# TensorE's program for RWKV pairs 1 to 7: a loop against a written-out program

## The reference, cut to what matters

```
xn = RMSNorm(h)
h += W_o( sigmoid(gA) * RWKV7(xn) + sigmoid(gB) * GLA(xn) )
h += SwiGLU(RMSNorm(h));  y = RMSNorm(h)

RWKV7, per head of 64 (16 heads), token by token:
S_t = S_{t-1} (diag(w_t) - kk_t^T (a_t * kk_t)) + v_t^T k_t ;  o_t = S_t r_t
```

## Time and profile before

| | |
|---|---|
| median of 3 runs | 2993.82 us (2993.78 to 2996.28) |
| the profiled execution | 2995.29 us, of which 2993.7 us span |
| TensorE busy | 2721.7 us, 91% of the span |
| VectorE, ScalarE busy | 928.4 us, 637.5 us |
| mean granted TensorE clock | 0.93 of full |
| RWKV pairs, from the first matmul of pair 0's inverse to that of pair 7's | 749.8 to 1857.9 us |

### The profile page before, as it was taken

How to read it: one execution, slowest core, us unless ns; L and a number is a source line. 1 busy time by engine, 2 the same in 40 slices (tenths; PEclk the granted TensorE clock), 3 DMA queues, 4 the chain that set the end, 5 groups by cost and what they waited for, 6 DMA issues and landing times.

```text
span 2993.7 us, 42715 instructions
## 1 busy us (share of the span) xinstructions
PE 2721.7 (91%) x17605; PEld 2108.0 (70%) x17605; DVE 928.4 (31%) x1682; ACT 637.5 (21%) x1001; POOL 19.1 (1%) x26
## 2 busy tenths in 40 slices
PE   5979797979999999999999999819699999999997
PEld 3656575756767676767676766719699999986665
DVE  1121212024445453536353535372311111100001
ACT  2211112122231322222222222121322222200001
POOL 0000000000000000000000000010000000000000
PEclk9989898979999999899999999759899999999999
DMA  3010101010000000000000000012011111110111
GB/s 132 20 58 14 58 14 64 8 45 1 30 2 30 2 30 2 30 2 30 1 8 24 2 30 2 29 43 106 7 49 47 44 49 42 49 72 20 39 39 57
DMA packets 19082, 99.58 MB, mean 33 GB/s; under 512 B 4544, under 2 KB 4736, under 8 KB 15120
## 3 DMA queue, kind: packets, MB, share of 16 engines
q1 hardware_dynamic: 17328, 88.44, 8.1%
q0 software_dynamic: 1632, 9.21, 0.8%
HBM read 86.31 MB, written 11.34 MB: 33 GB/s over the span
## 4 chain that ended last, share of the span: by engine, by line
PE 86%; DVE 9%; issue 3%; ACT 2%; DMA 0%; DVEq 0%; SPq 0%; ACTq 0%
PE banks L513 86%; ACT arena L883 1%; DVE arena L1446 1%; DMA arena<-in_consts 0%; DVE arena L1454 0%; DVE arena L1455 0%; DVE arena L1437 0%; DVE arena L1436 0%; DVE arena L1288 0%; DVE arena L1290 0%; DVE arena L1457 0%; DVE arena L1448 0%; DVE arena L1201 0%; DVE arena L1606 0%; ACT L883 0%
## 5 line engine op out<-in xcount | busy, mean ns | idle before, releaser
L513 PE MATMUL banks<-arena 64*64 64x64 f32 (+12 forms) x13826 | 2124.3, 329 | 227.2 <-DVE arena L1564 58.0
L513 PEld LDWEIGHTS banks<-arena 64*64 64x64 f32 (+3 forms) x13826 | 1511.1, 174 | 838.5 <-issue 413.8
L513 PE MATMUL banks<-merged_high,gate_up_high 128*128 128x344 f32 x1056 | 338.8, 321 | 23.5 <-DVE gate_up_low L1595 23.5
L513 PE MATMUL banks<-x_low,gate_up_high 128*128 128x344 f32 x1056 | 338.0, 320 | 0.0
L513 PE MATMUL banks<-merged_high,gate_up_low 128*128 128x344 f32 x1056 | 337.9, 320 | 0.0
L883 ACT ACTIVATE arena<-arena 128x64 f32<-128x64 f32 (+7 forms) x289 | 178.2, 634 | 657.9 <-DVE arena L1621 309.5
L513 PEld LDWEIGHTS banks<-merged_high,gate_up_high 128*128 128x128 f32 x1056 | 199.0, 188 | 24.1 <-issue 24.1
L513 PEld LDWEIGHTS banks<-merged_high,gate_up_low 128*128 128x128 f32 x1056 | 199.1, 189 | 0.0
L513 PEld LDWEIGHTS banks<-x_low,gate_up_high 128*128 128x128 f32 x1056 | 199.0, 188 | 0.0
L883 ACT ACTIVATE arena<-banks,arena 128x348 f32<-128x348 f32 (+3 forms) x180 | 97.0, 547 | 307.3 <-PE banks L513 298.3
L1595 DVE TENSOR_TENSOR gate_up_low<-arena,gate_up_high 128x1024 fp32r<-128x1024 f32 x44 | 53.8, 1225 | 310.4 <-ACT gate_up_high L1135 310.4
(11 more groups left out here) (140 smaller groups left out, 1109.6 us busy)
## 6 DMA issues: line engine op xcount, KB each, us to landing
arena<-in_w_gu SPq DMA_DIRECT2D x44, 512.0 KB, 3.7
arena<-in_w_pair SPq DMA_DIRECT2D x8, 2112.0 KB, 8.0
arena<-in_w_gla SPq DMA_DIRECT2D x4, 3072.0 KB, 9.6
arena<-in_w_d SPq DMA_DIRECT2D x7, 1408.0 KB, 6.1
arena<-in_xT SPq DMA_DIRECT2D x16, 516.0 KB, 7.2
out_yT<-arena SPq DMA_DIRECT2D x8, 516.0 KB, 3.0
arena<-in_gla_s POOLq DMA_DIRECT2D x4, 1024.0 KB, 5.0
out_glas<-arena POOLq DMA_DIRECT2D x4, 1024.0 KB, 4.1
```

Source lines behind the costliest of these rows:

```text
L513: return nc.tensor.matmul(out, lhsT, rhs, start=start, stop=stop)
```

## The change

TensorE's loop over the pairs becomes a loop of the program that writes the kernel, so that the body stands seven times in TensorE's instruction stream with i as a number. The other engines keep their loops. Nothing that is computed changes, nor the order of the matmuls, nor any semaphore.

```
-            with pe.Fori(1, NP) as i:
+            for i in range(1, NP):
                 for s in range(SLOTS):
                     chunk_step(i - 1, s // 3, s % 3)
                     for m in range(SPREAD):
                         if slot(m) == s:
                             projection(i, m)
                 chunk_products(i, True)
```

## The result

The changed kernel took 2954.45 us (median of 4 runs, 2948.29 to 2964.59) beside 2993.80 (4 runs, 2987.71 to 2996.28): ratio 0.9887, 95% interval 0.9854 to 0.992. The forecast was 2959, its range 2945 to 2967. The profiled execution took 2964.59 us, 30.7 less than that of before.

A forecast was written before the change was run, and what follows sets the result against it. TensorE, busy 91% of the span, was taken as the bound. From the profiled 2995.3 us, 34.5 for the jumps gave 2960.8, other terms unchanged; the median, 1.5 lower, was forecast at 2959, range 2945 to 2967.

The forecast's parts named there:

- The jumps go: Seams between TensorE's passes: without six jumps back, 34.54 us go, 10.3 of it idleness, the rest half-clock work and disturbed order.
- drops at the seams stay: Rival: the clock falls at seams without a jump too, only 6.6 us of idleness goes, time 2987; chance 0.08.
- half clock still follows the seams: Sign of being wrong: TensorE's granted clock was to be 1.00 behind each seam.
- The sign with the waits: At the seams, six waits of about 0.6 us for L1063 and 1.2 for L1377 replace six without releaser.
- The mid-pass drops: Clock drops after the L1457 wait before a pair's inverse: two kept, 13.15 us; bounds none or three (6.6 more).
- Instruction loading: TensorE's instruction queue: streaming the written-out code costs nothing; 11 or 12 packets a pass, total lower by about a dozen.
- The slower rival: Loading can't keep up at the ends of about 77 code blocks; if each stalled, time 3090; chance 0.02.
- Register arithmetic: TensorE's gates, whose expressions become constants: gain taken as nothing, at most 4.3 us over seven passes.
- The other engines' jumps: DVE and ACT keep their loop jumps: costed at nothing, some tenths of a us per seam if cover fails.
- The Trainium skill's rule on taken branches: A taken branch to a page not loaded stalls until it comes; alone it prices 10.3 us, time 2983.5.

The follow-up runs named there:

- The run with 34 waits: The changed kernel with 34 already satisfied semaphore waits at the start of passes 2 to 7, where the jump back stood: 2982.23 us, ratio 0.9988.
- the scan in four: The changed kernel with DVE's decay scan over 1024 columns cut into four of 256, the chunk's copies between them: 2937.19 us; in the kernel before: 2984.12.
- the turned loop: The kernel before, its loop body begun elsewhere, so all six jumps stand behind eight merge-gate matmuls and ahead of the L1457 wait: 2956.5 us, ratio 0.9889.
- the empty instructions: The changed kernel with 28 empty sequencer instructions at the start of passes 2 to 7, where the jump back stood: 2963.11 us, ratio 0.9907.
- the loops of one pass: The changed kernel with each of the seven written-out bodies in a loop of a single pass, meant to keep register arithmetic: 2964.38 us, ratio 0.9928.
- the kernels with 28 and 34 of them: The changed kernel with 28 or 34 already satisfied semaphore waits at the start of passes 2 to 7: 2978.81 us with 28, 2982.23 with 34.

## Why the prediction was right, and where it was not

*The jumps go.* Right that the idleness of the six seams goes, that the clock is the larger part of what a jump costs, and that L1063 and L1377 are late next. The run with 34 waits shows it: the same 10.3 us of idleness without a jump bring the same excess. The term was sized wrongly, though. I priced all six seams as the one of pass 1, "they did not bring the clock down", and so put 34.54 us down as gain. Three of the seven seams still had a drop, 11.54 us together, so this term came to 23.0 in the profiled execution. That is the step that failed: the seams without a jump were taken as free of clock drops on the word of one seam, and three of seven had one. It was given as a rival (drops at the seams stay) only for all six together, and "half clock still follows the seams" was a sign of being wrong that came true. The waits ahead of a seam are the same, 0.52 us for L1063 at six and 0.36 at the last, so they don't say which falls. In the profiles the clock fell behind 20 of 20 seams with 1.5 to 2.1 us of idleness, behind 5 of 6 with 1.0, behind 3 of 7 of the changed kernel with 0.5, and behind none of 14 with the same 0.5 us and the scan in four. What decides between 0.5 and 1.0 us is open; timing is the guess that fits. The sign with the waits came out in part too: 1.2 us for L1377 stood at four seams only.

*The mid-pass drops.* I kept two; there was one, 6.73 us, so this term gained 6.4 where I had nothing. The waits before the inverse are unchanged, 5.1 us in eight, as said. The number of drops over the variants' profiles is 0, 1, 2 or 3 with the same waits, so the waits don't decide it. The timing, the reason given, would fit, but was not controlled here.

*Instruction loading.* Right: two packets fewer per jump, no wait without a releaser in a program that crosses all its blocks in a row. The slower rival is out.

*Register arithmetic.* Right at nothing, by the turned loop, which has it all and the same distances; the run meant to test it did not have it. That no view shows these instructions was wrong: the view of L517 lists them, at 32 to 48 ns each.

*The other engines' jumps.* Right at nothing: undisturbed distances are 151.46 us while DVE, ACT, SP and POOL still jump.

*The sum.* For the profiled execution 34.5 was forecast and 30.7 measured: 23.0 + 6.4 within the pairs' stretch (1108.05 to 1078.50, 29.55 with rounding), and 1.1 outside. For the medians 34.5 was forecast and 39.4 measured in the first set, 28.3 and 20.2 in the two later sets. The two misses within the sum were of opposite sign. So the forecast number stood for a sum whose parts were off by 11.5 and 6.4, and that they partly cancelled is luck. So is what came on top: the median was put 1.5 us under the profiled execution, as before, and lay 10.1 under it. The profiled execution was 3.8 us above its own forecast of 2960.8, the median 4.5 below its 2959. All three medians of the changed kernel, 2954.45, 2963.04 and 2964.22, are within the range.

The Trainium skill's rule on taken branches (Runtime: NRT & Kernel Launch, instruction fetch mechanics) was put beside the rows with a time of 2983.5. Its stall is real here, 3.4 to 3.8 us in the record of each jump of this loop, but the case shows that the stall need not be seen at all: in the turned loop the same fetches are made and hidden.

## What to carry to other kernels

Where a loop's jump stands is a choice: put it right behind a run of matmuls that are issued without a wait, ahead of a point at which the engine waits anyway, and it can cost nothing, as here, where 6.6 us of queued matmuls covered a branch of 3.3 to 3.9 us; there is no need to write the program out for it. Price an idle gap of TensorE by taking the same stretch of work with and without it, not by its own length, since half clock behind it is in no list of waits and was two thirds of the cost here. Where two gaps compete for one place, the longer covers the shorter, and removing the shorter shows nothing until the longer is gone, as the scan in four did: 0 us with the jumps, 27 without, of which 8.7 are the gap itself. And look in the trace whether an experiment's edit is there: two of them here, the empty instructions and the loops of one pass, were not what their source said.

## What the runs showed of the hardware that was not expected

The spread of a kernel's timed runs goes with the clock: 3 to 31 us where drops can come and go (2978.36 to 3009.14 for the kernel before in one set, with mean clocks from 0.935 to 0.925), 2.1 and 2.5 us for the two kernels whose pairs run at full clock throughout. A profiled execution is not a random draw of these: the changed kernel's three profiles, and those of the turned loop, the empty instructions and the loops of one pass, had the same four drops. The changed kernel's took 2963.8 to 2964.6 us, the upper part of the timed runs.

The waits that are already satisfied start 0.11 to 0.13 us apart in the traces of the kernels with 28 and 34 of them, and six more made the idle time 0.73 us longer (0.97 to 1.70). That is how 34 of them stand in for a jump.

What a taken jump costs depends on the loop: the records of TensorE's branches back in the GLA loop, where no instruction packet came, are 0.21 to 0.25 us long, those of the loop over the pairs 3.4 to 3.8.
